# A hybrid decoder step on one core: the attention layer as one stream of 64 units with dense chunks between, and its bias tables copied through DRAM

## The reference, cut to what matters

```
kv = rmsnorm(x, kv_norm) @ w_kv                      # 4 K/V heads of 64
q  = rmsnorm(x, norm_mix[l]) @ w_q[j]                # 16 query heads, 4 per K/V head
s  = q . k * 64**-0.5 + bias                         # bias: T5 buckets of the distance, per head
m  = max(max(s), sink);  e = exp(s - m)              # window of 128 keys, one sink per head
p  = e / (sum(e) + exp(sink - m))
x  = x + (p . v) @ w_attn_out[j]
x  = x + relu(rmsnorm(x, norm_ffn) @ w_up)**2 @ w_down
```

## Time and profile before

| | us |
|---|---|
| median of 3 runs | 2665.02 (2660.18 to 2666.78) |
| the profiled execution, its span | 2668.29, 2666.3 |
| TensorE busy | 2511.0 (94%) |
| VectorE, ScalarE, GpSimd busy | 1227.8, 664.6, 145.8 |
| mean granted clock of TensorE | 0.961 of 2.4 GHz |

### The profile page before, as it was taken

How to read it: one execution, slowest core, us unless ns; L and a number is a source line. 1 busy time by engine, 2 the same in 40 slices (tenths; PEclk the granted TensorE clock), 3 DMA queues, 4 the chain that set the end, 5 groups by cost and what they waited for, 6 DMA issues and landing times.

```text
span 2666.3 us, 37243 instructions
## 1 busy us (share of the span) xinstructions
PE 2511.0 (94%) x15606; PEld 2374.0 (89%) x15606; DVE 1227.8 (46%) x2063; ACT 664.6 (25%) x1150; POOL 145.8 (5%) x141
## 2 busy tenths in 40 slices
PE   6899999988999999999998889878999999999998
PEld 6888888878999999999997668557999999999997
DVE  6545545566433333433364772674643343334332
ACT  3232222233211211121132440342321121112113
POOL 3000000012000000000020000001100000000002
PEclk8899999999999999999999898986999999999999
DMA  3111111111111111111113002000111111111111
GB/s 107 40 33 45 37 48 34 42 33 32 48 42 55 40 46 43 48 48 40 50 40 99 17 16 66 17 9 17 40 50 47 49 44 44 42 54 41 48 48 66
DMA packets 175204, 117.42 MB, mean 44 GB/s; under 512 B 23335, under 2 KB 170836, under 8 KB 175012
## 3 DMA queue, kind: packets, MB, share of 16 engines
q1 hardware_dynamic: 174900, 115.02, 14.7%
q10 hardware_dynamic: 144, 0.02, 0.0%
HBM read 107.86 MB, written 9.18 MB: 44 GB/s over the span
## 4 chain that ended last, share of the span: by engine, by line
PE 87%; DVE 8%; issue 2%; ACT 1%; DMA 1%; POOL 1%; SPq 0%; DVEq 0%; ACTq 0%
PE acc L1508 64%; PE acc L1583 5%; PE acc L1585 4%; PE acc L1584 4%; DVE prob L1363 1%; PE acc L1780 1%; PE acc L1792 1%; PE acc L1639 1%; PE acc L1606 1%; DVE w_lo L943 1%; DVE rstd L960 1%; PE acc L1804 1%; DVE stat L1366 1%; PE acc L1624 1%; PE acc L1667 1%
## 5 line engine op out<-in xcount | busy, mean ns | idle before, releaser
L1508 PE MATMUL acc<-x_hi,w_hi 128*128 128x352 f32 x1848 | 413.5, 332 | 21.5 <-DVE x_lo L949 11.2
L1508 PE MATMUL acc<-x_lo,w_hi 128*128 128x352 f32 x1848 | 402.7, 326 | 0.0
L1508 PE MATMUL acc<-x_hi,w_lo 128*128 128x352 f32 x1848 | 402.5, 326 | 0.0
L973 DVE TENSOR_TENSOR x_res<-x_res,acc 128x1056 f32<-128x1056 f32 x144 | 180.4, 1253 | 458.0 <-PE acc L1508 458.0
L1508 PEld LDWEIGHTS acc<-x_hi,w_hi 128*128 128x128 f32 x1848 | 315.5, 191 | 45.2 <-issue 40.1
L617 ACT ACTIVATE w_hi<-w_raw 128x1024 fp32r<-128x1024 f32 x180 | 189.3, 1051 | 627.4 <-PE acc L1508 577.3
L1508 PE MATMUL acc<-h_hi,w_hi 128*128 128x352 f32 x1536 | 332.1, 324 | 0.0
L1508 PE MATMUL acc<-h_hi,w_lo 128*128 128x352 f32 x1536 | 331.1, 323 | 0.0
L1508 PE MATMUL acc<-h_lo,w_hi 128*128 128x352 f32 x1536 | 330.6, 323 | 0.0
L1508 PEld LDWEIGHTS acc<-x_hi,w_lo 128*128 128x128 f32 x1848 | 321.2, 190 | 0.0
L1508 PEld LDWEIGHTS acc<-x_lo,w_hi 128*128 128x128 f32 x1848 | 318.5, 190 | 0.0
(11 more groups left out here) (262 smaller groups left out, 2697.7 us busy)
## 6 DMA issues: line engine op xcount, KB each, us to landing
w_raw<-in_w_up SPq DMA_DIRECT2D x64, 512.0 KB
w_raw<-in_w_down SPq DMA_DIRECT2D x64, 512.0 KB
w_raw<-in_w_mlstm_in SPq DMA_DIRECT2D x24, 512.0 KB
x_in<-in_x_prompt SPq DMA_DIRECT2D x8, 512.0 KB, 3.9
w_raw<-in_w_mlstm_out SPq DMA_DIRECT2D x8, 512.0 KB
w_raw<-in_w_q SPq DMA_DIRECT2D x16, 256.0 KB
w_raw<-in_w_attn_out SPq DMA_DIRECT2D x16, 256.0 KB
out_y_prompt<-y_out SPq DMA_DIRECT2D x8, 512.0 KB, 2.7
```

The source lines that it names most:

```text
L973: V.tensor_tensor(blocks(x_res[:, k]), blocks(x_res[:, k]), group(o), ALU.add).then_inc(out_taken, 1)
L1508: last = T.matmul(out[:, b], w[:, k, m], x[:, TN * b:TN * b + TN], start=(k == 0 and i == 0), stop=(k == k_chunks - 1 and i == 2))
```

## The change

The two groups, with their loops over heads, become one list of slabs (ATT), and the chunks of that list are dealt out to 64 units by a table:

```diff
+ATT = ([("kv", c) for c in (2, 3, 0, 1)] + [("q", n) for n in range(6)] + [("out", c) for c in range(4)] +
+       [("q", 6), ("q", 7)] + [("out", 4 + c) for c in range(4)])
+AFIRST = [sum(2 if kind == "out" else 1 for kind, _ in ATT[:p]) for p in range(len(ATT) + 1)]
+APLACE = {slab: p for p, slab in enumerate(ATT)}
+UNITS = (QH // 2) * NCH
+SAMPLE_AT = (23, 55)
+def att_window(u):
+    def place(u):
+        if u < 30:
+            return 43 + u
+        if u < 32:
+            return 72
+        if u < 37:
+            return min(80, 72 + 2 * (u - 31))
+        if u < 43:
+            return min(112, 80 + (16 * (u - 36) + 2) // 3)
+        if u < 47:
+            return 112 + 2 * (u - 42)
+        if u < 54:
+            return 120 + (8 * (u - 46)) // 7
+        return 128 + max(0, u - 63)
+    return range(place(u - 1), place(u))
```

So 42 chunks stand ahead of unit 0; units 0 to 29 have one each, 30 and 31 none, 32 to 35 two, 36 none, 37 to 42 five or six (the first group's output products), 43 to 46 two, 47 to 53 eight together, 54 to 63 none, and 29 chunks follow the last three steps, which have one each. TensorE's list, cut:

```diff
+            att_dense(range(19))
+            pe.wait_ge(blk_taken, BLK0 + 2 * TB)
...
+            x.then_inc(kvt_ready, 1)
+            att_dense(range(19, 35))
...
+            att_dense(range(35, 42))
+            scores(0)
+            for u in range(UNITS + 3):
+                if u + 1 < UNITS:
+                    scores(u + 1)
+                att_dense(att_window(u))
+                if 1 <= u <= UNITS:
+                    transposes(u - 1)
+                if 2 <= u <= UNITS + 1:
+                    values(u - 2)
+                for gp in range(2):
+                    sample(gp, u - SAMPLE_AT[gp])
+            att_dense(range(8 * APLACE["out", 4] + 3, 8 * len(ATT)))
```

Rows of dense output no longer take turns in two groups of three banks. Their blocks of 352 columns go round banks 0 to 3 one by one, and VectorE takes them out block by block; the scores have banks 4 and 5, the transposes bank 6 (two banks before), the values bank 7:

```diff
+                    for b in range(TB):
+                        g = BLK0 + TB * (AFIRST[p] + n) + b
+                        if kk == 0 and g >= BLK0 + 4:
+                            pe.wait_ge(blk_taken, g - 3)
...
+            def scores(u):
...
+                if u == 0:
+                    pe.wait_ge(kvt_taken, 2)
+                else:
+                    pe.wait_ge(mx_ready, u)
```

VectorE's maxima becomes one instruction per head that adds the bias, negates, and takes the minimum with the negated sink; the sink is put in as a 257th column of the score tile by GpSimd, so that the exponential's row sum has it:

```diff
+                for e in range(2):
+                    x = V.tensor_tensor_reduce(prob[:, r, e, lo:2 * WIN], acc[:, 4 + e, lo:2 * WIN], bias[:, 4 * e + n % 4, lo:],
+                                               -1.0, sinks[:, head + 4 * e:head + 4 * e + 1], ALU.add, ALU.min, stat[:, r, e:e + 1])
+                x.then_inc(mx_ready, 1)
...
+            for u in range(UNITS):
+                n = u // NCH
+                if u >= 2:
+                    pool.wait_ge(t_ready, u - 1)
+                nc.gpsimd.tensor_copy(prob[:, u % 2, :, 2 * WIN], by_head[:, n // 4, n % 4]).then_inc(sink_col, 1)
+                if u >= 11 and u % 8 == 3:
+                    o_low((u - 11) // 8, slice(0, SEQ), (u - 3) // 8)
```

The bias table is no longer turned on TensorE. During the first stage SP writes each head's row 128 times to DRAM, one copy behind each of 16 weight loads; later one load with a step of one column less than a row brings the turned table, and the second group's tables are loaded head by head over the first group's:

```diff
+                if 8 <= p < 8 + QH:
+                    h = p - 8
+                    if h == 0:
+                        sp.wait_ge(band_out, 16 * (1 + DEC_S))
+                    sp.dma_start(band_copies[h], dram("band", h * BAND, [[0, P], [1, BAND]])).then_inc(copies_out, 16)
...
+            def load_bias():
+                sp.wait_ge(att_go, 1)
+                sp.dma_start(sinks[:], dram("attn_sinks", 0, [[0, P], [1, QH]])).then_inc(bias_in, 16)
+                sp.wait_ge(copies_out, 16 * QH)
+                sp.dma_start(bias[:], copied(0, [[BAND - 1, P], [P * BAND, hq], [1, 2 * WIN]])).then_inc(bias_in, 16)
+            def reload_bias(h):
+                sp.wait_ge(mx_ready, 8 * (h + 1))
+                sp.dma_start(bias[:, h:hq:4], copied(hq + h, [[BAND - 1, P], [4 * P * BAND, 2], [1, 2 * WIN]])
+                             ).then_inc(bias_in, 16)
...
+                if p == 1:
+                    load_bias()
+                if p == 2:
+                    load_sample_bias(0)
+                if p == 4:
+                    load_cache(0)
+                if p == 6:
+                    store_kv()
+                if 8 <= p < 12:
+                    reload_bias(p - 8)
+                if p == 12:
+                    load_sample_bias(1)
+                    load_cache(1)
```

More of the change, by code:

```diff
@@ L798, in _, with att_dense @@
             mlp(0, KV)
-            for c in range(4):
-                split(At(S_KV + c + 1), At(O_KV + c))
-                if c == 0:
-                    root(2)
+            def att_dense(chunks):
+                for i in chunks:
+                    p, k = divmod(i, 8)
+                    if k == 0:
+                        if p > 0:
+                            act.wait_ge(blk_ready, BLK0 + TB * AFIRST[p])
+                        split(At(S_KV + p + 1), At(O_KV) if p == 0 else None)
@@ L865, in _ @@
+            for c in range(4):
+                att_dense(range(8 * APLACE["out", 4 + c] + (3 if c == 0 else 0), 8 * APLACE["out", 4 + c] + 8))
+                for k in (2 * c, 2 * c + 1):
+                    prepare(4, FFN1, k)
             mlp(1, None)
@@ new lines, in probabilities, with outputs @@
+            def probabilities(u):
+                r, lo = u % 2, WIN if u % NCH == 0 else 0
+                dve.wait_ge(ex_ready, u + 1)
+                V.reciprocal(stat[:, r, 4:6], stat[:, r, 2:4]).then_inc(dve_done, 1)
+                dve.wait_ge(dve_done, links.next)
+                for e in range(2):
+                    x = V.tensor_scalar(prob[:, r, e, lo:2 * WIN], prob[:, r, e, lo:2 * WIN], stat[:, r, 4 + e:5 + e], None, ALU.mult)
+                x.then_inc(pr_ready, 1)
+            def outputs(u):
+                n, b = divmod(u, NCH)
+                dve.wait_ge(o_ready, u + 1)
+                V.tensor_copy(q_t[:, n % 2, cols(b)], acc[:, 7, 0:P]).then_inc(o_taken, 1)
@@ L1318, in _ @@
+            mark(att_go)
+            V.memset(q_m[:], 0.0)
+            att_dense(range(4))
             mean_square(2)
             dve.wait_ge(rstd_ready, 3)
[L1320 to L1327 removed]
+            att_dense(range(4, 22))
@@ L1331, in _ @@
+            att_dense(range(28, 32))
+            for k in range(6, KD):
+                prepare(3, MIX1, k)
+            att_dense(range(32, 36))
+            dve.wait_ge(kvt_ready, 2)
             V.tensor_copy(v_tok[0:SAMP, NCH], acc[0:SAMP, 4, 0:256])
@@ new lines, in _ @@
+            att_dense(range(36, 42))
+            dve.wait_ge(sinks_set, 1)
+            for u in range(UNITS + 3):
+                if u < UNITS:
+                    maxima(u)
+                if 1 <= u <= UNITS:
+                    probabilities(u - 1)
+                if u >= 3:
+                    outputs(u - 3)
+                att_dense(att_window(u))
+                for gp in range(2):
+                    sample(gp, u - SAMPLE_AT[gp])
+            att_dense(range(8 * APLACE["out", 4] + 3, 8 * len(ATT)))
@@ new lines, in scores @@
+            def scores(u):
+                n, b = divmod(u, NCH)
+                gp, lo = n // 4, WIN if b == 0 else 0
+                if b == 0:
+                    pe.wait_ge(q_ready, n + 1)
+                if u == 0:
+                    pe.wait_ge(kvt_taken, 2)
+                else:
+                    pe.wait_ge(mx_ready, u)
+                for e in range(2):
+                    h = slice(HD * e, HD * e + HD)
+                    x = T.matmul(acc[:, 4 + e, lo:256], q_t[h, n % 2, cols(b)],
+                                 k_t[h, gp, P * b - P + lo:P * b + P], start=True, stop=True)
+                x.then_inc(s_ready, 1)
@@ new lines, in transposes, with values @@
+            def transposes(u):
+                r = u % 2
+                pe.wait_ge(pr_ready, u + 1)
+                if u >= 1:
+                    pe.wait_ge(tc_ready, u)
+                for e in range(2):
+                    for k in range(1 if u % NCH == 0 else 0, 2):
+                        at = P * (2 * e + k)
+                        x = T.transpose(acc[:, 6, at:at + P], prob[:, r, e, P * k:P * k + P], ident[:])
+                x.then_inc(t_ready, 1)
+            def values(u):
+                n, b = divmod(u, NCH)
+                r, k0 = u % 2, 1 if b == 0 else 0
+                pe.wait_ge(tc_ready, u + 1)
+                if u >= 1:
+                    pe.wait_ge(o_taken, u)
+                for e in range(2):
+                    g = HD * (2 * (n // 4) + e)
+                    for k in range(k0, 2):
+                        x = T.matmul(acc[HD * e:HD * e + HD, 7, 0:P], v_tok[:, b - 1 + k, g:g + HD],
+                                     prob_t[:, r, 2 * e + k], start=(k == k0), stop=(k == 1))
+                x.then_inc(o_ready, 1)
```

708 lines of the change are left out of this document (327 added, 381 removed).

## The result

The changed kernel takes 2569.8 us (median of 4 runs, 2562.1 to 2572.7) against 2665.2 (4 runs, 2660.2 to 2666.8): ratio 0.9641, 95% interval 0.9614 to 0.9667. The forecast was 2586. The profiled execution is the shortest of the four, 2562.05 us with a span of 2560.2. Its stretch, from the first K/V matmul at 1363.94 to the first of the second MLP at 1782.21, is 418.27 us where it was 510.55: 92.3 less, and 16.1 less than the 434.4 forecast. The stretch and the start of the first MLP (3.8 us less, e7) together make 96.1, the medians differ by 95.4. Between these two profiles the start and the mixer differ by 7.5 us more and what follows the second MLP's first matmul by about 2.5.

What follows compares the result with a forecast made beforehand. TensorE is 87% of the chain of waits, so only its lost or lower-clock time can be won. Terms summed to 434.4 us for 510.55, with the MLP 79.1 gained: forecast 2586 us, 8-in-10 range 2562 to 2630.

Steps and rivals of the forecast that it cites:

- dense and unit work: TensorE's work in the stretch: 160 dense chunks, 233.0 us, and the attention work of 64 units, 123.5 us.
- waits on the scores in units with chunks: Scores wait 0.43 us for VectorE's fused maxima in each of 51 units holding dense chunks: 21.9 us.
- VectorE's order: Evictions, output rows and splits queued on VectorE ahead of the next maxima make them late: 6 us.
- bare units: 13 units without dense chunks: 0.53 us each over the work, ten perhaps 0.5 more at 1.2 GHz; 11.9 us together.
- sample, TensorE and steps: Sample part, nine steps in units: 7 us of TensorE work a group and 6 for VectorE steps; 20.0 us.
- norm stall: Second K/V slab's second block waits for the norm: 6.9 us, plus 2.2 at 1.2 GHz; 9.1 us.
- end of the stream: Last outputs, up to GpSimd's low half and chunk 131: 5 us.
- rival A: VectorE's fused pair costs the full 1.38 us, 23 us more in 51 units: 2609 us; chance 0.13.
- the fusion costs 0.24 us a unit: Fused maxima hold the scores buffer longer, 0.24 us a unit; the change earns by having no drains.
- B: Rival: the stream of units with chunks falls to 1.2 GHz, about 117 us more: 2703 us; chance 0.05.
- C: Rival: VectorE's splits and evictions hold scores up 1.5 us in each of 26 cases: 2625 us; 0.15 together with D.
- D: Rival: a weight slab comes late on SP, at most 10.8 us for one, 2607 us for two; 0.15 together with C.

Runs made afterwards that it cites:

- e7: Changed kernel with the wait for all the mixer's evictions put back ahead of the first MLP: 2562.0 us, stretch 414.6 us.
- e2: Changed kernel with the fifth and sixth K/V block in banks 4 and 5, not waiting for the norm: 2554.8 us, stretch 405.4 us.
- e3: Changed kernel with three buffers for the probabilities instead of two: 2546.9 us, stretch 400.9 us.
- e1: Changed kernel with the pipeline emptied again between the eight heads: 2586.2 us, stretch 440.8 us.
- e10: Changed kernel with the sample's nine steps done in two lumps per group instead of one per unit: 2588.8 us, stretch 443.9 us.
- e5: Changed kernel with the fused maxima undone into an addition, a reduction and a small minimum: 2576.9 us, stretch 428.3 us.
- e4: Changed kernel with the 30 chunks of the first 30 units done eight at once in one unit per head: 2568.1 us, stretch 420.1 us.
- e9: Kernel with e2's and e3's edits, VectorE's maxima and probabilities ahead of evictions and splits only in units without sample steps: 2527.0 us, stretch 380.6 us.
- e11: Kernel of e5 with GpSimd's low half of a head's outputs held back until that unit's probabilities are scaled: 2579.0 us, stretch 429.8 us.

## Why the prediction was right, and where it was off

**The sum.** To compare terms I added up, over TensorE's rows of the stretch, the time from each row's start to the next one's, less the wait ahead of that next row.

| term | forecast | measured |
|---|---|---|
| dense and unit work | 356.5 | 241.4 + 114.6 = 356.0 |
| waits on the scores in units with chunks; VectorE's order | 21.9 + 6 | 21.6, and 0.9 at the very first |
| bare units | 11.9 | 3.3, and 1.2 for probabilities |
| sample, TensorE and steps | 20.0 | 19.5 + 0.8 |
| K/V transposes and the norm's sums | 4.0 | 3.7 |
| norm stall, and its half-speed part | 6.9 + 2.2 | 6.75, rest in the work; e2: 9.1 |
| end of the stream | 5 | 1.9 |
| dense blocks waiting for VectorE | none | 2.7 |

The work came out to 0.5 us and the stall in place, cause and size. For the work that is in part luck: some 5 us of the 356.0 (an estimate from the rows that began at 1.2 GHz) are time at the lower clock, of which the forecast had 2.2 in the stall's term; at full speed the work would be some 5 us under it. (The change of operand, some 6 us, stands in the dense rows here and in the unit work there.) In the sample's row, too, the total agrees by luck: TensorE's work was 19.5 for 14, the steps 0.8 for 6. The wait of 0.43 was 0.40 and is what e3 takes away: the mechanism, the fused pair standing behind the transposes, is shown. The prediction worked it out from the pair's length and did not name the buffer for which the pair waits. The fused instruction is 0.48, an addition's 0.43 and little more, so rival A is out. The halved rate that the Trainium skill (Vector Engine (DVE) Microarchitecture Reference, Points that are easy to get wrong) gives for two SBUF sources did not show, in line with its condition, since one source is in PSUM.

The 16 us too many are margins that the profile did not claim. Bare units: I gave them waits of 0.53 and a cold clock of 0.5, but in units 56 to 63 the sample's steps stand in the gap ahead of the scores, work that I had counted by itself and not as cover. The clock stayed at 1.00 in units 55 to 61. VectorE's order: its 6 us are inside the 21.6, since ten units don't wait at all. And the end of the stream took 1.9, not 5.

**Where the 92 us came from.** The prediction named drains, the unit's waits, the sample, the flip and the clock, and priced the result, not each part. The runs price some: the drains 22.5 (e1), the sample's interleaving 25.6 (e10), the fused maxima 10.0 (e5). Dealing the chunks out singly (e4) is no part of it, since the kernel before did so too. The flip's products are in the trace before as 7.3 us of TensorE:

```profile
L1832 PE MATMUL acc<-bias,flip 128*128 128x512 f32 x16 | 7.3, 597 | 1.4 <-DVE x_res L973 1.4
```

That is 65 of 92, or, with e10 at 29.3, 77 of 96 against e7's stretch, if the parts add up, which wasn't tried. The rest is not priced; what wasn't undone alone are the waits for the turned table, the clock of the old last head, the wider products of the sample.

The traces split the 92 us in another way. TensorE's waits fell by 43 (82 to 39), its rows by 49 (428.4 to 379.2 us, added up as in the table). The mean clock of the stretch before is in this line; after it was 0.98:

```profile
1375.28:1885.83 510.55, 428.40 (x2679) 353.80 (x2677) 298.71 (x743) 171.26 (x457) 36.76 (x16) 0.88 0.13 35
```

Rows that began at 1.2 GHz fell from 96.7 to 17.8 us. At the ratio of the matmuls behind the norm stall, which start 0.29 us apart and 0.16 at full speed, that is worth some 36 us, an estimate. So waits, clock and flip make 86 of the 92. Drains and lumps bring the lower clock back with the waits: such rows are 31.8 us in e1 and 42.2 in e10.

One step of the prediction failed outright: that the fusion costs 0.24 us a unit and earns nothing in the stream. It does hold the score banks longer, but e5 shows that without it the stretch is 10 us longer.

**The rivals.** B: the clock was 1.00 in units 0 to 29 and from 34 on, and most of e4's bare units kept it too. The forecast's sign, 1.00 from unit 0 to 53, failed in units 30 to 33, which ran at 0.50 to 0.90; in e7 only unit 33 was below 1.00. C: units 6, 14 and 22 are 0.5 longer than the others, not 1.5 in each of 26; e9 wins 5.1 us there and at units 47 and 54. D: no wait of TensorE on a weight split stands in the stretch. The first MLP's 3 us were 3.8, just outside the bound of 3.7.

## What to carry to other kernels

Ask of each short, regular wait which buffer its instruction stands behind; here 0.40 us before most of 64 scores was one tile of 2 KB a partition, worth more than the fused instruction. A unit's gap is covered only by work that stands in the gap, in program order: the sample's steps stood there, the dense chunks did not. Where runs scatter by 10 us and more, price a part by undoing it and reading its own stretch of the profile, and first see by how much that stretch differs between two executions of the same instructions.

## What the runs showed of the hardware

- VectorE's scalings from SBUF to SBUF waited for a GpSimd subtraction that had begun before them: 2.69 us instead of 0.62, seven times in e5, none in e11. The Trainium skill, SBUF — State Buffer, SBUF: two separate sides, says that VectorE and GpSimd share a pair of ports which whichever starts first holds for its whole instruction, against VectorE's two-port modes or (where the GpSimd instruction reads SBUF) two SBUF inputs. The trace agrees; that these scalings run in such a mode no run here shows.
- A fused instruction with a result per row is two rows in the trace, 0.48 and 0.08, and the next begins at the start of the read: 0.41 a step for 256 columns.
- The granted clock differs between executions with the same instructions in the same order: unit 30 took 11.76 us at 0.76 in the changed kernel and 9.45 at 1.00 in e2. In the stretch this is 3.7 us between the changed kernel and e7.
